# Three MoBA pairs scored and multiplied during input panels 11 to 13, a ring of three pairs, and MoBA's join in the middle of the column stage

## The reference, cut to what matters

```
A  GLU -> causal depthwise conv (width 31) -> LayerNorm -> swish -> pointwise product
B  sparse attention: compressed blocks, selected blocks (top 16), sliding window; mixed by gates
C  MoBA, 4 heads: blocks of 256 keys, gate = q . mean(k), top 3 blocks plus the own one
D  trailing means over 2, 4, 8, 16 rows minus the row, linear map, scale
x = LN(alpha * x + concat(A, B, C, D) @ w_out);  x = LN(alpha * x + relu(x @ w_up)^2 @ w_down)
```

## Time and profile before

| what | value |
|---|---|
| median of three runs | 766.1 us |
| the profiled execution: time, span | 767.9 us, 766.2 us |
| TensorE, VectorE, ScalarE, GpSimd busy | 738.0, 428.7, 285.0, 210.4 us |
| granted TensorE clock, mean | 0.99 |
| DMA moved | 113.5 MB, mean 148 GB/s |
| input panels with NSA, panels 13 to 16, column stage, rest | 0 to 143.8, to 227.6, to 326.7, to 766.2 us |

### The profile page before, as it was taken

How to read it: one execution, slowest core, us unless ns; L and a number is a source line. 1 busy time by engine, 2 the same in 40 slices (tenths; PEclk the granted TensorE clock), 3 DMA queues, 4 the chain that set the end, 5 groups by cost and what they waited for, 6 DMA issues and landing times.

```text
span 766.2 us, 17341 instructions
## 1 busy us (share of the span) xinstructions
PE 738.0 (96%) x6904; PEld 658.9 (86%) x6904; DVE 428.7 (56%) x740; ACT 285.0 (37%) x559; POOL 210.4 (27%) x284
## 2 busy tenths in 40 slices
PE   8999999998989999799999999999999999999997
PEld 8999989875554455499999999999999999999996
DVE  4778994665653532647865556434563355536355
ACT  5222324465563322524434554212341134324115
POOL 0000527014237761004647722001110012100434
PEclk9999999999998999989999999999999999999999
DMA  9656774388789997122333323322233322325002
GB/s 329 182 160 180 203 203 111 118 291 300 275 295 321 257 283 247 61 85 66 126 138 92 97 88 110 111 83 84 87 106 94 101 79 88 111 83 165 2 15 99
DMA packets 63980, 113.49 MB, mean 148 GB/s; under 512 B 17017, under 2 KB 36218, under 8 KB 63226
## 3 DMA queue, kind: packets, MB, share of 16 engines
q1 hardware_dynamic: 57370, 95.58, 40.1%
q0 software_dynamic: 6528, 16.78, 6.7%
HBM read 107.90 MB, written 6.52 MB: 149 GB/s over the span
## 4 chain that ended last, share of the span: by engine, by line
PE 78%; DVE 9%; DMA 5%; issue 4%; ACT 3%; POOL 1%; SPq 0%; POOLq 0%; ACTq 0%; DVEq 0%
PE psum L795 55%; PE psum L814 4%; PE psum L822 3%; PE psum L901 3%; DMA moba_lo<-in_moba_pages 2%; PE psum L935 2%; DMA moba_hi<-in_moba_pages 2%; PE psum L1099 2%; PE psum L870 1%; PE psum L1087 1%; DVE yc L1702 1%; DVE wL L1632 1%; DMA wgate<-in_w_gate 1%; DVE oxL L2056 1%; PE psum L1152 1%
## 5 line engine op out<-in xcount | busy, mean ns | idle before, releaser
L1632 DVE TENSOR_TENSOR wL<-raw,wH 128x1024 fp32r<-128x1024 f32 (+1 forms) x85 | 107.1, 1261 | 84.0 <-ACT wH L1260 83.9
L1260 ACT ACTIVATE wH<-raw 128x1024 fp32r<-128x1024 f32 (+1 forms) x87 | 88.8, 1021 | 105.8 <-PE psum L795 103.2
L795 PE MATMUL psum<-oxH,wH 128*128 128x260 f32 (+1 forms) x512 | 105.0, 286 | 0.7 <-DVE oxL L2056 0.5
L795 PE MATMUL psum<-oxH,wL 128*128 128x260 f32 (+1 forms) x512 | 103.9, 284 | 0.0
L795 PE MATMUL psum<-oxL,wH 128*128 128x260 f32 (+1 forms) x512 | 103.4, 283 | 0.0
L1594 POOL TENSOR_TENSOR hsq<-relu 128x520 f32<-128x520 f32 x32 | 33.8, 1056 | 217.9 <-ACT relu L1439 217.9
L795 PE MATMUL psum<-opH,wH 128*128 128x260 f32 x400 | 86.4, 298 | 4.8 <-DVE wL L1632 1.4
L795 PEld LDWEIGHTS psum<-oxH,wH 128*128 128x128 f32 x512 | 79.5, 189 | 2.5 <-issue 1.6
L795 PE MATMUL psum<-opH,wL 128*128 128x260 f32 x400 | 81.1, 284 | 0.0
L795 PE MATMUL psum<-opL,wH 128*128 128x260 f32 x400 | 80.8, 284 | 0.0
L795 PEld LDWEIGHTS psum<-oxL,wH 128*128 128x128 f32 x512 | 79.9, 190 | 0.0
(11 more groups left out here) (395 smaller groups left out, 1310.2 us busy)
## 6 DMA issues: line engine op xcount, KB each, us to landing
raw<-in_panels SPq DMA_DIRECT2D x88, 512.0 KB, 3.6
nsa_ring<-in_nsa_pages SPq DMA_DIRECT2D x128, 96.0 KB, 2.2
moba_hi<-in_moba_pages SPq DMA_DIRECT2D x36, 256.0 KB, 5.4
moba_lo<-in_moba_pages SPq DMA_DIRECT2D x36, 256.0 KB, 5.1
moba_hi<-in_moba_pages POOLq DMA_DIRECT2D x28, 256.0 KB, 5.0
moba_lo<-in_moba_pages POOLq DMA_DIRECT2D x28, 256.0 KB, 5.4
xres<-in_xT SPq DMA_DIRECT2D x8, 260.0 KB, 5.6
xres<-in_xT SPq DMA_DIRECT2D x1, 2080.0 KB, 8.8
```

The source lines that it names most:

```text
L795: last = mm(out[:, hf, 0:cols], w, x[:, k, hf * HALF:hf * HALF + cols], start=(t == 0 and j == 0), stop=(t == KT - 1 and j == 2))
L1260: fn(wtiles(0, n).rearrange("p a b -> p (a b)")[:, cols], raw[:, n % NRAW, cols], ACT.Copy).then_inc(h_done, 1)
L1632: tt(wtiles(1, n).rearrange("p a b -> p (a b)")[:, cols], raw[:, n % NRAW, cols], wtiles(0, n).rearrange("p a b -> p (a b)")[:, cols].bitc ...
```

## The change

- Pairs 0, 1 and 2 (`EP = 3`) are done early: pair 0 between the quarters of panel 11, pair 1 behind panel 12 and the eighth `nsa`, pair 2 between the pieces of panel 13. Their pages go to spare places (`hole`, `ahead_z` in slots of zT not yet written, `ahead_v` over Vn and zs, `ring0`). GpSimd issues the first 12 pages behind the first `pdiff`; SP the next 12 behind the loads for the eighth compression, after `mp` of pair 0. Their results go to `OM_early` and are copied to OM later.
- Pairs 3 to 11 (`MB1 = 12`) take the places that pairs 0 to 8 had in panels 14 to 16, with a ring of three pairs; pair 3's pages are loaded as soon as the eighth compression has scored. winV is loaded after pair 11. Pairs 12 to 15 remain in the column stage, each with 8 groups of selV pages.
- `pool` 0 goes ahead of `cmean`; `pool` 1 and the two `cpw` go behind pair 1's steps, `cpw` 1 to the other pair of banks; panels 11 and 12 use pair 1 of the banks.
- MoBA's join starts at key 37.4 (`join_`) instead of `end`. `end` stays at 64.7. The last copies to zT and the splits of the mixer outputs get earlier keys.

```diff
-MB1, PAIR_T, SELV_T = 9, 9.1, 6
+MB1, PAIR_T, SELV_T = 12, 9.1, 8
+EP = 3
+BUF = [None] * EP + [(0, 1, 2)[(_n - EP) % 3] for _n in range(EP, MB1)] + [(_n - MB1) % 2 for _n in range(MB1, MB)]
+NEXT = {_n: min(_m for _m in range(_n + 1, MB) if BUF[_m] == (2 if _n == EP - 1 else BUF[_n])) for _n in range(EP - 1, MB - 2) if _n != MB1 - 1}
...
-            return (out + m[:1] + [("kv", B)] + m[1:3] + [("csc", 0)] + m[3:4] + [("zcols", 0)] + m[4:6] + r[:1] + m[6:7] + r[1:2] + m[7:8]
-                    + [("evac", i)] + extras + r[2:])
+            return (out + m[:1] + [("kv", B)] + m[1:2] + [("mu", 2)] + m[2:4] + [("csc", 0), ("mt", 2)] + m[4:5] + [("zcols", 0), ("mp", 2)] + m[5:6]
+                    + r[:1] + m[6:7] + r[1:2] + m[7:8] + [("evac", i)] + extras + r[2:])
...
+            if i == 11:
+                at_ = step.index(("mm", 11))
+                step[at_:at_ + 1] = [("mm", 11, 0, 4), ("mu", 0), ("mm", 11, 1, 4), ("mm", 11, 2, 4), ("mt", 0), ("mm", 11, 3, 4), ("mp", 0)]
+            if i == 12:
+                step.append(("mu", 1))
...
-        if i == ATT_PANEL - 1:
-            tl.append(("pool", 1))
...
+            if b == B - 2:
+                tl.append(("early", 1))
...
-            tl += [("out_early", 0), ("pdiff", 0)]
+            tl += [("out_early", 0), ("pdiff", 0), ("early", 0)]
...
-            tl += [("cmean", 0), ("pool", 0), ("pdiff", 1), ("qm", 0), ("out_conv", 0)]
+            tl += [("pool", 0), ("cmean", 0), ("pdiff", 1), ("qm", 0), ("out_conv", 0)]
...
-            tl += [("cpw", 0), ("load_lo", 0)]
+            tl += [("mt", 1), ("pool", 1), ("mp", 1), ("cpw", 0), ("cpw", 1), ("load_lo", 0)]
...
-    units = []
+    units = [(1.5, ("load_winV", 0))]
...
-    end = 1 + PAIR_T * (MB - MB1)
+    end = 64.7
...
+    join_ = 1 + PAIR_T * (MB - MB1)
+    last = [(join_, ("statm", 0)), (join_ + 0.1, ("combm", 0)), (join_ + 6.5, ("combe", 1)), (join_ + 8, ("combm", 1)), (join_ + 9.5, ("combm", 2)), (join_ + 12, ("backm", 0)), (join_ + 15.5, ("mpv", 0)),
+            (join_ + 19, ("finm", 0)), (end + 8, ("msplit", 6)), (end + 25, ("msplit", 7))]
...
-PAIR = [1 if NACC0 <= n < NACC1 else n % 2 if n < NACCF else (0, 1, 3)[(n - NACCF) % 3] for n in range(len(ACC))]
+NACCE = ACC.index(("mm", 11))
+PAIR = [int(ACC[n] not in (("cvar", 0), ("cpw", 1))) if NACCE <= n < NACC1 else (n + NACCE + 1) % 2 if n < NACCE else n % 2 if n < NACCF else (0, 1, 3)[(n - NACCF) % 3] for n in range(len(ACC))]
...
+        hole = place("moba_hole", [P, 4, 512], F32, o_a + 8192)
+        ring0 = place("moba_ring0", [P, 4, 512], F32, o_a + 16384)
+        ahead_z = place("moba_z", [P, 4, 512], F32, o_z + S_MK * NT * 4)
...
+            if n < EP:
+                return ((hole, ahead_z), (ahead_v, ahead_z), (hole, ring0))[n][e]
+            return (moba_hi[:, e], moba_lo[:, e], (hole, ring0)[e])[BUF[n]]
...
                 elif kind == "load_post":
                     sp_.wait_ge(ssel_mm, B)
+                    load_unit(EP, 0, moba_in[0])
+                    sp_.dma_start(winK[:, :, :], a["winK"]).then_inc(win_in, 16)
+                    load_unit(EP, 1, moba_in[0])
...
-                    load_unit(0)
-                    load_unit(1)
+                elif kind == "early" and n == 1:
+                    sp_.wait_ge(mp_mm, 1)
+                    load_unit(1, 1, early_hw)
+                    load_unit(2, 0, early_hw)
+                    sp_.wait_ge(ssel_mm, B - 1)
+                    load_unit(2, 1, early_hw)
...
+                if kind == "early" and n == 0:
+                    pool.wait_ge(ids_in, 16)
+                    for m, e in ((0, 0), (0, 1), (1, 0)):
...
+                    if n < EP:
+                        pe.wait_ge(early_hw if n else early_sw, 192)
```

More of the change, by code:

```diff
@@ L306 @@
         ACC.append(_s)
[L307 removed]
+    if _s[0] in ("pool", "cmean", "cvar", "cpw") or _s == ("gate", 1):
         ACC.append(_s)
[L309 to L310 removed]
 NACC1 = ACC.index(("mm", OUT0))
@@ L350 @@
         USES[_b].append(_s)
+USED_BEFORE, ACC_BEFORE = {}, {}
+_seen, _last = [0] * 4, [None, None]
+for _s in TL:
+    _key = ("mm", _s[1]) if _s[0] == "mm" else _s
+    if _key in ACC_NO and _key not in USED_BEFORE and PAIR[ACC_NO[_key]] in (0, 1):
+        _p = PAIR[ACC_NO[_key]]
+        USED_BEFORE[_key] = {_b: _seen[_b] for _b in (2 * _p, 2 * _p + 1)}
+        _last[_p] = _key
+    for _b in range(4):
+        if _s in USES[_b]:
+            ACC_BEFORE[_b, _s] = _last[_b // 2]
+            _seen[_b] += 1
 def nth(bank, step):
@@ L477, in build, with unit, loaded @@
         wgate = place("wgate", [P, KT * GW], F32, o_vn)
+        XR = place("XR", [P, QT, P], F32, o_vn + 2048)
+        ahead_v = place("moba_v", [P, 4, 512], F32, o_vn + 2048)
+        OM_early = place("OM_early", [P, EP, HD], F32, o_vn + 10240)
+        own_early = place("own_early", [P, 256], F32, o_vn + 10240 + EP * HD * 4)
+        def unit(n, e):
+            if n < EP:
+                return ((hole, ahead_z), (ahead_v, ahead_z), (hole, ring0))[n][e]
+            return (moba_hi[:, e], moba_lo[:, e], (hole, ring0)[e])[BUF[n]]
+        def loaded(n, e):
+            by_pool = sum(m >= EP + 2 and BUF[m] == BUF[n] for m in range(EP, n + 1))
+            by_sync = sum(1 + (m < EP + 2) for m in range(EP, n + 1) if BUF[m] == BUF[n])
+            if e and n >= EP + 2:
+                return moba_odd[BUF[n]], 64 * by_pool
+            return moba_in[BUF[n]], 64 * by_sync
         zs = place("zs", [B, 12, P])
@@ L563, in build @@
         nsa_in = [sem(f"nsa_in{i}") for i in range(2)]
-        moba_in = [sem(f"moba_in{i}") for i in range(4)]
+        moba_in = [sem(f"moba_in{i}") for i in range(3)]
+        early_sw, early_hw = sem("first_pages_by_gpsimd"), sem("early_pages_by_sync")
         win_in, state_in, masks_in = sem("win_in"), sem("state_in"), sem("masks_in")
@@ L599, in build @@
         mixh, mixl = sem("mixh"), sem("mixl")
-        moba_odd = [sem(f"moba_odd_pages{i}") for i in range(2)]
+        moba_odd = [sem(f"moba_odd_pages{i}") for i in range(3)]
         gate_in, gate_mm, raw0_first = sem("gate_weights_in"), sem("gate_mm"), sem("raw0_first_half_in")
@@ L626, in pages, with load_unit @@
                     page_ids[0:1, first:first + n], [mybir.EngineType.SP])[1]
-            def load_unit(q, ids=None):
-                for p, v in enumerate(ids or pages(q * 4, 4)):
-                    sp_.dma_start(moba_ring[q % 4][:, p, :],
-                                  a["moba_pages"][bass.ds(v, 1)].rearrange("a p n -> (a p) n")).then_inc(moba_in[q % 4], 16)
+            def load_unit(n, e, done, ids=None):
+                for p, v in enumerate(ids or pages(8 * n + 4 * e, 4)):
+                    sp_.dma_start(unit(n, e)[:, p, :],
+                                  a["moba_pages"][bass.ds(v, 1)].rearrange("a p n -> (a p) n")).then_inc(done, 16)
             for kind, n, *part in TL:
@@ L737, in acc_wait @@
                     read(pe, ACC[last[-1]])
+                if NACCE <= n < NACC1:
+                    for k, uses in USED_BEFORE[key].items():
+                        if uses > (USED_BEFORE[ACC[last[-1]]][k] if last else 0):
+                            pe.wait_ge(bfree[k], uses)
                 if n == NACCF + 2:
@@ L942, in bank @@
                     pe.wait_ge(bfree[k], n)
-                else:
-                    read(pe, ACC[max(m for m in range(NACC1) if PAIR[m] == k // 2)])
+                if ACC_BEFORE[k, step] and (n == 0 or ACC_BEFORE[k, step] != ACC_BEFORE[k, USES[k][n - 1]]):
+                    read(pe, ACC_BEFORE[k, step])
             pe.wait_ge(const_done, 1)
@@ L1033, in _ @@
                 elif kind == "cpw":
-                    pe.wait_ge(cswish, 2)
-                    for m in range(2):
-                        acc_wait(("cpw", m))
-                        for hf in range(2):
-                            for t in range(2):
-                                last = mm(acc(("cpw", m))[:, hf, 0:HALF], vec[:, V_PW + t * 256 + m * P:V_PW + t * 256 + (m + 1) * P],
-                                          yc[:, t, hf * HALF:(hf + 1) * HALF], start=(t == 0), stop=(t == 1))
-                        last.then_inc(cpw_mm, 1)
+                    if n == 0:
+                        pe.wait_ge(cswish, 2)
+                    acc_wait(step)
+                    for hf in range(2):
+                        for t in range(2):
+                            last = mm(acc(step)[:, hf, 0:HALF], vec[:, V_PW + t * 256 + n * P:V_PW + t * 256 + (n + 1) * P],
+                                      yc[:, t, hf * HALF:(hf + 1) * HALF], start=(t == 0), stop=(t == 1))
+                    last.then_inc(cpw_mm, 1)
                 elif kind == "csc":
```

85 lines of the change are left out of this document (42 added, 43 removed).

## The result

The changed kernel takes 761.65 us, the median of five runs (759.45 to 762.96), the kernel before 767.23 beside it; the ratio is 0.992 (0.990 to 0.995). A second set on another occasion gave 762.95 (760.05 to 765.01) and 0.993 (0.990 to 0.996). So the change is worth 4 to 6 us. The forecast was 758.2, a gain of 7.9.

A forecast was written before the change was run, and what follows sets the result against it. TensorE, busy 96% of the span, was taken as the bound, so only its waits and low clock could pay. Removed 17.3 minus added 9.4 gave 7.9 us: profiled 767.9 to 760.0, median 766.1 to 758.2; range 751 to 764.

The forecast's parts named there:

- Moved work is worth nothing: Three pairs (6.75 us) into panels 11 to 13, and MoBA's join (4 to 5 us) within the column stage: cancels.
- Removed 1 to 3: Page waits gone in panels 14 to 16 (4.2 us) and before the column stage's first pair (3.0), low clock behind (2.9).
- Removed 4 and 5: Column stage's end: idle before the output projection (4.0 us), small waits (1.25) and low clock behind (2.0) go.
- Added 1: Panel 11: starts 0.1 us earlier, of a 1.3 us wait; pair 0's scores lose 0.2 us while QM is written.
- Added 2: Panels 12 and 13: waits on VectorE at pairs 1 and 2, less waits removed there; net 3.45 us lost.
- Added 3: Low clock behind pair 1's waits in panels 12 and 13: 3.0 us lost, bounds 0 and 3.7.
- Added 4: Middle of column stage: 1.3 us for Om in the join, 0.7 for pair 15's pages; together 2.0, bounds 0 and 8.
- rival C: Column stage: pages of pairs 14 and 15 late behind selV pages, waits 4.0 and 3.1 us, clock falls; 771.1 us, chance 0.07.
- the prediction's own signs of being wrong: TensorE waiting for pages in panel 11 or at pairs 14 and 15, or the mid-stage join stopping it over 2 us.
- Added 5: Last four columns: ScalarE, with 8.7 us of work, sets the pace of the stage's last 10 us; 1.0 us lost.
- rival A: Panels 12 and 13: clock holds or VectorE is not late, and half the mid-stage loss goes; 753.5 us, chance 0.29.
- the added side, 9.4: All forecast losses together, from panel 11 through panels 12 and 13 to the column stage's last columns: 9.4 us.

The follow-up runs named there:

- the kernel with the better orders: Changed kernel with pair 1 reordered, four smaller waits covered and two ScalarE evacuations put before exponentials: 753.27 us, ratio 0.980 to the kernel before.
- the last two kernels: Changed kernel with pair 1, small waits and ScalarE evacuations reordered, 753.27 us; the same with pair 0's scores behind five eighths of panel 11, 752.41 us.

## Why the prediction was right or wrong

The sign and the mechanism were right, and so were the places of the waits in the profile after; the gain is 4.2 to 5.6 us in the two sets where 7.9 were forecast. By its steps:

- *Moved work is worth nothing*: not tested by itself. That two parts which move nothing of it, the ring and the join's place, cost 12.3 and 3.9 to 5.2 us when undone leaves no sign of a gain from the moved work.
- *Removed 1 to 3 (the ring, 10.1)*: all gone in the profile after. Undone, the ring cost 12.3 us, and 6.8 to 8.5 in the kernel with the better orders. That 10.1 lies among these sizes is in part luck, as the places were not right: beside three early pairs the waits of a ring of two are 2.8 us in panels 14 to 16 and 8.1 at pairs 13 to 15. I had priced the ring by where the waits stood before, when six groups of selV pages went with a pair, not eight. A new wait of 0.7 us for zs stands before pair 12; I had not seen it behind the wait for pages.
- *Removed 4 and 5 (the join, 7.25, less 1.3 in the middle)*: the gap and the low clock went as forecast. The gap was 3.5 us of idle time and not 4.0: TensorE was busy for 4.09 of the 7.62 us between the two starts of the earlier trace rows. The price is 4.9 us by the medians and 6.7 by the ratios, where 5.95 were forecast. Of the low clock a part lies over a wait (5.08 of 6.0 us busy between 315 and 321), where TensorE had nothing to do.
- *Added 1 (gain of 0.1, loss of 0.2)*: 0.2 gained before panel 11 (1.1 instead of 1.3), but 1.1 us lost for QM. I had taken QM's four copies on VectorE to end when they did before, in 1.6 us; they took 2.5. GpSimd's adds of the trailing means ran beside them in both kernels, and a copy that starts while such an add runs ends only with it. Before, that was one copy (114.30 to 115.35, the add 114.29 to 115.32); after, two (113.61 to 114.49, the add 113.43 to 114.46; and 114.69 to 115.97, the add 114.69 to 115.94). The others took 0.2 us.
- *Added 2 (3.45)*: the transpose waited 1.55 (2.2 forecast), pair 1's product 1.73 (1.95), pair 2's 0.4 (0.7), and the 1.2 for zT are gone: 3.7 instead of 4.85. A wait that I had left out is pair 1's pages, 0.5 us: its semaphore also counted pair 2's.
- *Added 3 (3.0)*: the step with the wrong certainty. In the first profiled run the clock was low for 3.4 us, which cost 1.6 us beside the second, where it did not fall here, nor did it with the join at the end; in three other experiments with these waits it was low for 7 us. It is a chance with a price between 0 and some 3.5, not a price. "TensorE: Matmul & The Clock Gate" in the Trainium skill (HAM oscillation) puts the penalty at half of the throttled time, an estimate of 1.7 us for the first of these. The trace's 1.6 agrees.
- *Added 4 (2.0)*: Om held the next transpose of the selected probabilities (L1190) for 1.1 (1.3 forecast). The pages of pairs 14 and 15 cost 1.5 us in the first profiled run and 3.0 in the second, with low clock behind it, where 0.7 were forecast. That is rival C's mechanism at a fifth to two fifths of its 7.1 us, and its cure confirms it: SP's queue. It is also one of the prediction's own signs of being wrong. The 9.9 us for sixteen selV pages were right (9.7), and the pages took 3.8 us from the last issue to landing where 5 were forecast. But SP was done with pair 15's load 28.4 us after pair 12's scores instead of 26.7 (235.64 to 264.04), as it also waits for its turns; in the second run the four pages alone took it 2.8 us instead of 1.9. And pair 14, at the same queue, was not in the sum.
- *Added 5 (1.0)*: did not show: in the window that answers to the earlier trace rows TensorE is busy throughout while ScalarE has 8.3 us of work.

```profile
306.60:319.50 12.90, 12.90 (x196) 7.35 (x194) 4.47 (x9) 8.34 (x19) 0.00 (x0) 1.00 0.60 208
```

Two numbers of the prediction do not follow from its rows: the gap of 4.0 above, 0.5 too much in the sum, and the time of rival A, whose own terms (3.0, half of 3.45, half of 2.0) give 752.5 and not 753.5.

What was mis-sized is the added side, 9.4: too small by the waits that it left out or made short (QM 0.9, pair 1's pages 0.5, zs 0.7, pairs 14 and 15 by 0.8 to 2.3), too large by the clock (3.0 where 1.6 and 0 were seen). The profiled run of after had the small ends of those, so that its 8.5 us look like the forecast is luck, and the medians are what counts.

## What to carry to other kernels

Price a wait together with the low clock that may stand behind it: the gap before the output projection had 3.2 us of waits and some 6.8 us at 1.2 GHz from 324 us on, and moving the join away brought 5 to 7 us. A load that must be early is only as early as its place in the issuing queue: 16 small pages are 10 us of issue. And when the times of one kernel spread over several us, look for waits of 1 to 2 us on TensorE with low clock behind them in some profiles: covering them bought 8 us and made the spread smaller (5.0 us for eight runs; 0.5 and 2.4 us for five of the last two kernels).

## What was not expected of the hardware

The same waits did or did not drop the clock. Of 1.4 and 1.6 us at pair 1, the run with the ring of two made 7 us at 1.2 GHz (146 to 153), and the second profile of the changed kernel none; 1.55 and 1.73 us were followed by 3.4 us. The wait of 1.1 us for Om was followed by some 3.5 us of low clock in two of the kernels and by none in the others. The stretches came as some 3.5 or some 7 us in all the profiles: the two of before, read in windows of 1 us, are 6.8 us each. So such a term belongs into the range of a forecast, with a chance, and not into its sum.

SP's issue is not cheap beside the transfer: sixteen pages of 32 KB took it 9.7 us. The Trainium skill ("DMA: Bandwidth & Descriptors", Issuing engines are not separate DMA queues) calls what an issuing engine spends on this usually small; here it was what delayed pair 15: putting the load ahead of eight of the small pages removed its wait, though the bytes on the engines stayed the same.

A short VectorE copy (64 x 8, 0.2 us alone) that started beside a GpSimd add lasted until the add ended, 0.9 to 1.3 us, in the profiles of before and after. In the kernel after, TensorE waited 1.1 us for these copies before pair 0.
